# Four 512x1024x1024 products of a hybrid decoder made of seven half-size products each

## What is computed

```
def rwkv7_time_mix(...):
    ...
    return ((o + bonus).astype(h.dtype) * g) @ w_o          # recurrence output

def moba_attention(h, positions, w_qkv, w_o):
    qkv = (h @ w_qkv).reshape(B, T, 3, N_HEADS, HEAD_DIM)   # queries, keys, values
    q = jnp.transpose(rotary(qkv[:, :, 0], positions), (0, 2, 1, 3))
    k = jnp.transpose(rotary(qkv[:, :, 1], positions), (0, 2, 1, 3))
    v = jnp.transpose(qkv[:, :, 2], (0, 2, 1, 3))
    ...
    return o @ w_o                                           # MoBA output

x = x + mixed
x = x + mem_cross_attention(...)
x = x + hierarchical_moe(...)
```

## Time and profile before

| | |
|---|---|
| median of 3 runs | 2415.26 us (2414.26 to 2416.35) |
| the profiled execution | 2417.4 us, its span 2415.8 us |
| PE busy | 2079.1 us, 86% of the span |
| DVE busy | 614.5 us, 25% |
| ACT busy | 410.4 us, 17% |
| POOL busy | 196.6 us, 8% |
| mean granted TensorE clock | 0.951 of full speed |

### The profile page before, as it was taken

How to read it: one execution, slowest core, us unless ns; L and a number is a source line. 1 busy time by engine, 2 the same in 40 slices (tenths; PEclk the granted TensorE clock), 3 DMA queues, 4 the chain that set the end, 5 groups by cost and what they waited for, 6 DMA issues and landing times.

```text
span 2415.8 us, 32993 instructions
## 1 busy us (share of the span) xinstructions
PE 2079.1 (86%) x14168; PEld 1069.1 (44%) x14168; DVE 614.5 (25%) x1330; ACT 410.4 (17%) x983; POOL 196.6 (8%) x238
## 2 busy tenths in 40 slices
PE   6999999899998788778775999999998787878773
PEld 3434999874455332222222444546455322222221
DVE  6034555461033211000102321711033111010003
ACT  1033233320121000000001003610121000000001
POOL 1000211020000111111100000000000111110110
PEclk9999899999998899999998999999998999999997
DMA  4210000212144799999996121014254799999995
GB/s 141 97 43 9 3 4 4 90 71 104 70 176 155 304 408 400 407 402 405 410 408 247 70 70 70 1 53 139 70 188 157 303 404 409 410 405 409 399 410 202
DMA packets 113070, 515.07 MB, mean 213 GB/s; under 512 B 20736, under 2 KB 21896, under 8 KB 95536
## 3 DMA queue, kind: packets, MB, share of 16 engines
q1 hardware_dynamic: 101824, 496.34, 52.4%
q0 software_dynamic: 10880, 16.81, 2.1%
q10 hardware_dynamic: 240, 0.07, 0.0%
HBM read 503.73 MB, written 28.31 MB: 220 GB/s over the span
## 4 chain that ended last, share of the span: by engine, by line
PE 66%; DMA 22%; DVE 5%; SPq 4%; ACT 2%; issue 1%; POOLq 0%; DVEq 0%; POOL 0%; ACTq 0%
DMA big<-in_moe_w 20%; PE ps L1694 11%; PE ps L2130 11%; PE ps L1681 10%; PE ps L1788 9%; PE ps L2058 5%; SPq L479 4%; PE ps L2151 4%; PE ps L1743 2%; PE ps L2023 1%; PE ps L1928 1%; PE ps L2035 1%; PE ps L1889 1%; PE ps L1934 1%; PE ps L1955 1%
## 5 line engine op out<-in xcount | busy, mean ns | idle before, releaser
L2130 PE MATMUL ps<-big 128*64 128x512 f32 x2048 | 476.2, 619 | 76.9 <-DMA big<-in_moe_w 73.7
L2130 PEld LDWEIGHTS ps<-big 128*64 128x64 f32 x2048 | 163.0, 142 | 341.0 <-issue 329.3
L2151 PE MATMUL ps<-big 128*64 128x512 f32 x1024 | 252.5, 638 | 31.2 <-ACT big L1041 31.2
L1694 PE MATMUL ps<-big 128*128 128x512 f32 x640 | 275.4, 592 | 0.0
L1681 PE MATMUL ps<-big 128*128 128x512 f32 (+1 forms) x640 | 251.0, 555 | 6.1 <-DVE big L1117 6.1
L1788 PE MATMUL ps<-big 64*64 64x64 f32 (+1 forms) x6144 | 207.7, 225 | 12.0 <-issue 6.4
L1788 PEld LDWEIGHTS ps<-big 64*64 64x64 f32 x6144 | 202.2, 137 | 15.0 <-issue 6.8
L1694 PEld LDWEIGHTS ps<-big 128*128 128x128 f32 x640 | 121.4, 190 | 151.9 <-issue 151.8
L1681 PEld LDWEIGHTS ps<-big 128*128 128x128 f32 x640 | 122.4, 192 | 132.4 <-issue 127.0
L1573 DVE SCALAR_TENSOR_TENSOR big<-big,ps 128x256 f32<-128x256 f32 x64 | 26.9, 421 | 534.1 <-ACT big L1034 534.1
L2151 PEld LDWEIGHTS ps<-big 128*64 128x64 f32 x1024 | 72.6, 145 | 169.8 <-issue 131.3
(11 more groups left out here) (316 smaller groups left out, 1878.9 us busy)
## 6 DMA issues: line engine op xcount, KB each, us to landing
big<-in_moe_w SPq DMA_DIRECT2D x192, 2048.0 KB, 33.8
big<-in_mx_wkv SPq DMA_DIRECT2D x8, 2048.0 KB, 8.0
big<-in_rw_wrkv SPq DMA_DIRECT2D x6, 2048.0 KB, 7.9
big<-in_mb_wqkv SPq DMA_DIRECT2D x6, 2048.0 KB, 8.0
big<-in_mx_wq SPq DMA_DIRECT2D x4, 2048.0 KB, 7.9
big<-in_mx_wo SPq DMA_DIRECT2D x4, 2048.0 KB, 8.1
h_rows<-big SPq DMA_DIRECT2D x16, 512.0 KB, 12.1
big<-y_rows SPq DMA_DIRECT2D x8, 1024.0 KB, 8.3
```

The costliest lines, as they stand in the source:

```text
L1694: ins = mm(d[:], lhsT=lhs[:, k, t * P:(t + 1) * P], rhs=w[:, k, :], start=k == 0, stop=k == KT - 1)
L2130: ins = mm(ps[2 + b][half * BR:(half + 1) * BR, :], lhsT=hgT[b][:, k], rhs=w13[set_][:, :, k, half * 256:(half + 1) * 256], start=k == 0, ...
L2151: ins = mm(ps[5 + b][half * BR:(half + 1) * BR, :], lhsT=hT[b][:, c0:c0 + BR], rhs=w2[set_][:, f, half * HB:(half + 1) * HB], start=f == 0 ...
```

## The change

rwkv_out, mk, mv and moba_out are no longer made by `to_tokens` but by `in_seven` (Strassen's scheme in Winograd's form). The left operand is cut into a11, a12, a21, a22 (256 tokens by 512 channels), the weight into b11, b12, b21, b22 (512 by 512). DVE makes four sums of left quarters (s1 to s4, 128x1024 each, in the region of XN) and four sums of weight quarters (t1 to t4, 128x2048 each, in place). PE makes seven products of 256 x 512 x 512 in the order 1, 2, 6, 4, 7, 5, 3, each as two fills of four matmul calls, so 56 calls and 14 fills for a stage. DVE adds each fill to the one to four places of the result that need it. Product 1 of mk and mv is copied out twice by ACT; the keys are now turned from SBUF, after the sums, not from PSUM. mk and mv share the left sums. Weights are loaded in quarters, so a stage's pair of halves is four DMAs of 1 MB. After one of the four stages, the next pair's quarters are issued as sums and products free them. The norms after rwkv_out and moba_out wait for product 3.

```diff
+PRODUCTS = (1, 2, 6, 4, 7, 5, 3)
+    seven = lambda s: [(s, m, i) for m in PRODUCTS for i in range(2)]
...
-    o += [("gn_t", p, half) for p in range(PAIRS) for half in range(2)] + both("rwkv_out")
+    o += [("gn_t", p, half) for p in range(PAIRS) for half in range(2)] + seven("rwkv_out")
...
+            def load(j, h):
+                rows = slice(4 * h, 4 * h + 4)
+                sp.dma_start(W[j % 2][:, rows], loads[j][0][:, rows]).then_inc(w_loaded[j % 2][h], 16)
+
+            def load_pair(j):
+                last = PAIR[j // 2 - 1] if j else None
+                if last in SEVEN:
+                    n = SEVEN.index(last)
+                    sp.wait_ge(weight_sums, 4 * n + 4)
+                    load(j, 0)
+                    wait_filled(sp, (last, 7, 1))
+                    load(j + 1, 0)
+                    wait_filled(sp, (last, 5, 1))
+                    load(j, 1)
+                    wait_filled(sp, (last, 3, 1))
+                    load(j + 1, 1)
+                    return
+                for i in range(2):
+                    if j:
+                        wait_filled(sp, loads[j - 2 + i][1])
+                    for h in range(2):
+                        load(j + i, h)
...
-                    wait_emptied(act, ("rwkv_out", 1, t))
+                    wait_emptied(act, ("rwkv_out", 3, t % 2))
...
+            def side_first(u):
+                V.tensor_tensor(s3, a11, a21, ALU.subtract).then_inc(side_sums, 1)
+                dve.wait_ge(side_sums, 4 * u + 1)
+                V.tensor_tensor(s2, a22, s3, ALU.subtract).then_inc(side_sums, 1)
+                dve.wait_ge(side_sums, 4 * u + 2)
+            def side_last():
+                V.tensor_tensor(s4, a12, s2, ALU.subtract).then_inc(side_sums, 1)
+                V.tensor_tensor(s1, s2, a11, ALU.add).then_inc(side_sums, 1)
+            def t3(s):
+                count = 16 * (PAIR.index(s) + 1)
+                for h in range(2):
+                    dve.wait_ge(w_loaded[1][h], count)
+                V.tensor_tensor(b12, b22, b12, ALU.subtract).then_inc(weight_sums, 1)
+            def t2(s):
+                n, count = SEVEN.index(s), 16 * (PAIR.index(s) + 1)
+                dve.wait_ge(w_loaded[0][0], count)
+                wait_filled(dve, (s, 1, 1))
+                dve.wait_ge(weight_sums, 4 * n + 1)
+                V.tensor_tensor(b11, b12, b11, ALU.add).then_inc(weight_sums, 1)
...
+                side_first(u)
+                t3(s)
+                for i in range(2):
+                    add(1, i, (i, lo), (i, hi), (2 + i, lo), (2 + i, hi))
+                t2(s)
+                side_last()
+                for i in range(2):
+                    add(2, i, (i, lo))
+                t4(s)
+                for i in range(2):
+                    add(6, i, (i, hi), (2 + i, lo), (2 + i, hi))
+                t1(s)
...
+                for i in range(2):
+                    product(1, i, part(0, 0, i), b11)
+                pe.wait_ge(w_loaded[0][1], count)
+                for k in range(4, KT):
+                    ready(k)
+                for i in range(2):
+                    product(2, i, part(0, 1, i), b21)
+                pe.wait_ge(weight_sums, 4 * n + 2)
+                pe.wait_ge(side_sums, 4 * u + 2)
+                for i in range(2):
+                    product(6, i, summed(2, i), b11)
+                pe.wait_ge(weight_sums, 4 * n + 3)
+                for i in range(2):
+                    product(4, i, part(1, 1, i), b21)
+                for i in range(2):
+                    product(7, i, summed(3, i), b12)
+                pe.wait_ge(weight_sums, 4 * n + 4)
+                pe.wait_ge(side_sums, 4 * u + 4)
+                for i in range(2):
+                    product(5, i, summed(1, i), b21)
+                for i in range(2):
+                    product(3, i, summed(4, i), b22)
...
-            to_tokens(("rwkv_out",), HT, gn_ready)
+            in_seven("rwkv_out", gn_ready)
```

More of the change, by code:

```diff
@@ L76, in bank_group_order @@
         if l == 1:
-            o += mix_order() + [("mq", 1, t) for t in range(TT)] + both("mk") + both("mv") + per("mqT") + per("mkT")
+            o += mix_order() + [("mq", 1, t) for t in range(TT)] + seven("mk") + seven("mv") + per("mqT") + per("mkT")
             n += 1
-            o += moba_order() + both("moba_out")
+            o += moba_order() + seven("moba_out")
         if l == 1:
@@ L413, in trunk @@
             USE.setdefault(last[:-1] if last[0] in ("r", "k", "xk", "xq") else last[:-1], []).append(j)
+        PAIR = [loads[j][1][0] for j in range(0, len(loads), 2)]
+        b11, b21, b12, b22 = (region(4 + i)[:, h * 2048:(h + 1) * 2048] for i in range(2) for h in range(2))
+        side = [region(1)[:, i * 1024:(i + 1) * 1024].rearrange("p (k q) -> p k q", k=4) for i in range(4)]
         def load_index(stage, half):
@@ new lines, in _, with ready, to_residual, add @@
+            lo, hi = slice(0, HB), slice(HB, C)
+            def ready(s, m, i):
+                wait_filled(dve, (s, m, i))
+                if m != 1:
+                    wait_emptied(dve, (s, PRODUCTS[PRODUCTS.index(m) - 1], i))
+            def to_residual(s, u):
+                def add(m, i, *parts):
+                    ready(s, m, i)
+                    for t, cols in parts:
+                        ins = V.tensor_tensor(x[:, t, cols], bank((s, m, i))[:], x[:, t, cols], ALU.add)
+                    empties(ins, (s, m, i))
+                side_first(u)
[11 more added lines that the diff above has]
+                for i in range(2):
+                    add(4, i, (2 + i, lo))
+                for i in range(2):
+                    add(7, i, (2 + i, lo), (2 + i, hi))
+                for i in range(2):
+                    add(5, i, (2 + i, hi), (i, hi))
+                for i in range(2):
+                    add(3, i, (i, hi))
@@ new lines, in to_rows, with add @@
+            def to_rows(s, dst, rotate):
+                def add(m, i, *parts):
+                    ready(s, m, i)
+                    for (t, cols), (t_in, cols_in) in parts:
+                        ins = V.tensor_tensor(dst[:, t, cols], bank((s, m, i))[:], dst[:, t_in, cols_in], ALU.add)
+                    empties(ins, (s, m, i))
+                same = lambda t, cols: ((t, cols), (t, cols))
+                t3(s)
+                t2(s)
+                for i in range(2):
+                    add(2, i, same(i, lo))
+                t4(s)
+                for i in range(2):
+                    wait_emptied(dve, (s, 2, i))
+                    add(6, i, ((i, hi), (2 + i, lo)))
+                    rotate(i, 0)
+                t1(s)
+                for i in range(2):
+                    add(4, i, ((2 + i, lo), (i, hi)))
+                for i in range(2):
+                    add(7, i, ((2 + i, hi), (i, hi)), same(2 + i, lo))
+                for i in range(2):
+                    wait_emptied(dve, (s, 7, i))
+                    rotate(2 + i, 0)
+                    add(5, i, same(2 + i, hi), same(i, hi))
+                for i in range(2):
+                    wait_emptied(dve, (s, 5, i))
+                    rotate(2 + i, 1)
+                for i in range(2):
+                    add(3, i, same(i, hi))
+                for i in range(2):
+                    wait_emptied(dve, (s, 3, i))
+                    rotate(i, 1)
@@ L1300, in _ @@
                         unstacks(dve, V.tensor_copy, p, half)
-            for half in range(2):
-                for t in range(TT):
-                    add_out(("rwkv_out", half, t), half, t)
+            for p in range(PAIRS):
+                for half in range(2):
+                    wait_emptied(dve, ("gn_t", p, half))
+            to_residual("rwkv_out", SUMS["rwkv_out"])
             for l in range(2):
@@ L1368, in _ @@
                     weighted(PAIRS - 1)
-                    for half in range(2):
-                        for t in range(TT):
-                            add_out(("moba_out", half, t), half, t)
+                    for p in range(PAIRS):
+                        wait_emptied(dve, ("mo", p))
+                    to_residual("moba_out", SUMS["moba_out"])
                 if l == 1:
```

149 lines of the change are left out of this document (96 added, 53 removed).

## The result

Median of the changed kernel 2389.62 us (2388.89 to 2390.19, four runs), of the kernel before beside it 2415.81 us (2414.26 to 2419.40, four runs). The ratio is 0.9889, 95% interval 0.9872 to 0.9906: 26.2 us faster, by the interval 22.7 to 30.9. The profiled execution took 2390.18 us, its span 2388.4 us, at a mean granted TensorE clock of 0.952.

What follows compares the result with a forecast made beforehand. The prediction took PE's record count to bound the four dense stages: 27.47 us removed, less 0.9 of wait and 0.3 for fill boundaries, is 26.3 us; 2415.26 - 26.3 = 2389.0 us, range 2386.0 to 2395.0.

Steps and rivals of the forecast that it cites:

- two quarters landed: mk: both 1 MB quarters of W[1] land 8.2 us after issue, 8.0 at least, 9.6 at most.
- t2 ends in mk: mk: weight sum t2 ends at 1393.9, product 6 due at 1394.6; wait 0, at the upper end 1.1 us.
- t2 ends in mv: mv: weight sum t2 ends some 9.7 us into the stage, 13.7 allowed; wait 0.
- t2 ends in moba_out: moba_out: weight sum t2 ready at 1593.0 to 1593.9, product 6 due at 1593.7; wait 0 to 0.2, taken 0.
- What was removed: Four dense stages: 64 to 56 calls each, 16 records less at 0.4292 us; 6.87 us a stage, 27.47 us in all.
- The wait in rwkv_out: rwkv_out: PE waits before product 6 for DVE's weight sum t2; 0.3 to 1.5 us, taken 0.9.
- The 0.3 us for fill boundaries: Four dense stages: PE's own waits grow from 8 to 14 fills a stage; 0.3 us allowed for all.
- Behind the stages: After rwkv_out: the norm's squares come some 2.4 us later, with 22 us of cover; no wait of its transposes.
- Small gaps at every product: Rival, four stages: 56 products' semaphore waits cost 0.1 us each, 5.6 us come back; 2394.3 us; chance 0.10.
- Kept elsewhere: Rival, expert stages: loads that don't move with PE swallow layer 0's 6.0 us or all, up to 2415; chance 0.03.
- Slow sums: Rival, four stages: DVE's sums of two SBUF operands slower by 2.65, waits of 49.5 us; 2437 us; chance 0.04.
- More comes back than 27.5 us: Rival, expert stages: shifted starts let one wait less; 2385 us or so; chance 0.05.

Runs made afterwards that it cites:

- calls added: Changed kernel with both fills of product 3 running their four matmul calls twice, so 64 calls a stage again; 2416.87 us, ratio 0.9997 to the kernel before.
- the layer-0 run: Changed kernel with only rwkv_out in seven products, the other three stages' code as before; 2410.25 us, ratio 0.9969 to the kernel before.
- the two POOL runs: Changed kernel with sums added on POOL beside rwkv_out: 24 of 128x1024, 2399.14 us; 48 of 128x512, 2393.78 us.
- the run with three sums: Changed kernel with each of the 16 weight sums computed two extra times into a spare region; 2436.36 us, ratio 1.0078 to the kernel before.
- POOL in halves: Changed kernel with 48 sums of 128x512 added on POOL beside rwkv_out, in place of 24 of 128x1024; 2393.78 us.
- sums twice: Changed kernel with each of the 16 weight sums computed one extra time into a spare region; 2408.77 us, ratio 0.9956 to the kernel before.

## Why the prediction was right

Forecast 2389.0 us (2386.0 to 2395.0), measured 2389.62. Times from a stage's start, from the prediction's working and from the trace:

| step | predicted | measured |
|---|---|---|
| one record | 0.4292 us | 0.4292 |
| saved in keys and values | 13.74 | 13.75 |
| saved in moba_out | 6.87 | 6.87 |
| product 6 late in rwkv_out | 0.3 to 1.5, took 0.9 | 0.34 (0.18 shown as idle) |
| extra fill boundaries, all | 0.3 | none seen |
| weight sum of 2048 | 2.29 | 2.27 to 2.29 |
| two quarters landed | 8.2 | 7.9 (t3 starts) |
| t2 ends in mk | 13.1 | 12.6 |
| t2 ends in mv | 9.7 | 10.1 |
| t2 ends in moba_out | 13.1 to 14.0 | 12.7 |

**What was removed** is right to the hundredth where no wait stands, and shown by itself: with the 64 calls back, the gain goes (2416.87 us).

**The wait in rwkv_out** was the term that was mis-sized: I took 0.9 us from 0.3 to 1.5. The profile shows 0.18 of idle time, but product 6 begins 539.91 - 525.83 = 14.08 us after the stage's first record, where it was due after 13.74: 0.34 late, at the lower end. The stage lost 0.45 in all. In the working, each own-semaphore wait could cost 0.1 us and each add up to 0.69. In the trace s3 and s2, with such a wait behind each, are followed 1.26 us later (duration 1.23), t3 is followed 2.21 us later by the adds (duration 2.29), and the adds stand 0.60 apart, so the lower choice held at each place. The prediction weighed the Trainium skill, "VectorE: DVE Perf Modes", section "The DRAIN you can't avoid", against the rows; by the prediction's reading of it the adds stand 0.69 apart. Here too 0.60 was measured, and the rows' value decides. The section's last sentence, which the prediction did not weigh, says that an operation that isn't held starts earlier; the 0.60 is no contradiction to that.

**The 0.3 us for fill boundaries** was not needed, by the keys and values with calls added. So the stages gave 27.5 - 0.45 = 27.0 us where the prediction's sum had 26.3. The profiled executions differ by 2417.4 - 2390.2 = 27.2; the medians differ by 26.2, and the interval of the ratio holds all of these. That the forecast fell within 0.6 us of the median is in part luck of the runs.

**Where the time arrives.** rwkv_out's share goes through the experts of layer 0, as the chain was read: the layer-0 run kept 6.9 us with one stage. The span fell by 27.4 us, 0.4 more than the stages gave. Parts that no edit touches differ by more from run to run: rwkv_out begins between 524.22 and 526.25 us in the ten profiled kernels, whose matmuls are the same up to there, and the stretch behind it differs by 3.6 us. So the 0.4 us can't be told from chance.

**Behind the stages** nothing waits longer, as predicted: the memory values begin at 574.51 in the chain, and the transposes behind them 27.47 us later without a gap. Behind moba_out PE waits 1.54 us for DVE's scaling of the memory rows, before and after.

**The rivals.** Small gaps at every product: ruled out (109.87 us for 256 records in 28 fills). Kept elsewhere: ruled out by layer 0 alone. Slow sums: didn't occur, since POOL was at rest; its mechanism is real, but its price was wrong, as the two POOL runs show: turns, not a factor. Its sum of 49.5 us also left out slack that the prediction itself had: by its own times product 6 would wait 10.6 us in moba_out, 7.0 in mk and 3.6 in mv, 47 us in all. Its estimate that a factor of about 2 decides was of the right size. Weight sums at twice their time still leave 8.3 us of gain, at three times 19.3 are lost; the line between crosses zero near 2.3, with left sums at their own price. But its sum left out what a wait does to the clock, 5.0 and 10.9 us in these two runs. More comes back than 27.5 us: not seen.

## What to carry to other kernels

Where one engine has no gap, as PE here, its instruction count prices the change, and the rest is a question of when each helper result is ready: a list of the helper's operations from the stage's start, at the distance between neighbours (0.60 us here for an add of 0.69), gave the slack of four stages within 0.5 us. Check such slack by adding a known piece of work and reading the waits, and count behind every wait of some microseconds the slower matmuls too. Keep POOL's sums of SBUF operands out of a stretch where DVE's are awaited, or cut them short, since DVE may stand for the whole of one.

## What the runs showed of the hardware

- The granted clock fell from 1.00 to half (0.50) while PE waited: in the run with three sums it is 1.00 in the window 530 to 538, 0.65 in 538 to 546 and 0.50 in 546 to 550. Behind the waits before product 6 of 4.2 us and more the first window shows 0.50 to 0.60, and the 16 records behind three of them took 8.65, 8.70 and 9.52 us for 7.0.
- Behind two shorter waits it had fallen too (0.57 behind 2.92 us in POOL in halves, window 542 to 546, and 0.57 behind 3.48 us with sums twice, window 1395 to 1399), with a smaller loss (36.25 us for 80 records where 34.60 is usual, 49.80 for 112 where 48.2 is). Behind 3.43 us in moba_out with sums twice it was 1.00 (window 1588 to 1592) and nothing was lost (16 records in 7.13 us), nor behind the 1.03 us before mv's product 6. What decides between 2.9 and 3.5 us is open.
- DVE and POOL take turns by whole instructions when both read two SBUF operands. A DVE add with one operand in PSUM is not held up (eight in 4.86 us beside POOL and without).
- Two 1 MB loads in place of one of 2 MB changed the time by nothing that could be measured (ratio 0.9999, 0.9990 to 1.0009).
